# Two-layer transformer step, one core: the order of the matmuls of a pair of 64-wide heads in neighbourhood attention

## The chip, the core and the metric

The kernel runs on one core of one Trainium2 chip, in float32 throughout (many matmuls take float32 values that were rounded to the chip's fp32r form). The metric is device time in microseconds, the median of several executions; lower is better.

## The reference, cut to what matters

The program computes a first block (spatial gating, sparse attention, cross attention to a memory, feed-forward) and then a second block of two layers on a latent sequence `x` of 512 rows and a context `ctx` of 256 rows. The change touches only the attention of the second block: 8 heads of width 64. Each query of the latent grid (8 rows of 64 columns) sees a band of its grid neighbours and all 256 context rows; in layer 0 the context also attends to itself.

```python
def context_attention(q, k, v):
    s = jnp.einsum('bqhd,bkhd->bhqk', q, k, preferred_element_type=jnp.float32) * (NA_HEAD_DIM ** -0.5)
    p = jax.nn.softmax(s, axis=-1).astype(v.dtype)
    return jnp.einsum('bhqk,bkhd->bqhd', p, v).reshape(B, L, NA_CH)

def row_block(r):          # neighbourhood_attention, one grid row of queries
    ...
    s_loc = jnp.einsum('bjqhd,bijkhd->bhjqik', q_r, k_b,
                       preferred_element_type=jnp.float32) * scale + bias
    s_ctx = jnp.einsum('bjqhd,bchd->bhjqc', q_r, k_ctx,
                       preferred_element_type=jnp.float32) * scale
    s = jnp.concatenate([s_loc.reshape(B, NA_HEADS, nj, NA_QC, n_loc), s_ctx], axis=-1)
    p = jax.nn.softmax(s, axis=-1).astype(v.dtype)
    p_loc = p[..., :n_loc].reshape(B, NA_HEADS, nj, NA_QC, kh, NA_KB)
    o = (jnp.einsum('bhjqik,bijkhd->bjqhd', p_loc, v_b)
         + jnp.einsum('bhjqc,bchd->bjqhd', p[..., n_loc:], v_ctx))
```

## The kernel before, in words

The program is written as five instruction streams, one for each engine, by five functions that walk through the same stages in the same order; semaphores tie them together. The order on each engine is the order of the code. Most of the program on TensorE is large projections: a weight tile is split into a high and a low fp32r part (`hib` and `lob`), the activations likewise (`Hh` and `Hl`), and three matmuls (high by high, low by high, high by low) make one product. All matmuls go through the helper `mm` (line 816) and all transposes through `turn` (line 819), so the profile puts nearly all of TensorE's work on these two lines, and the tiles' names tell them apart.

The change lies in `near_attention` of TensorE's stream (line 1413). The work there is cut into pairs of heads: `hp` is one of four pairs of heads, `j` one of four blocks of 128 queries for the latent (`s == "x"`), or one of two for the context (`s == "c"`). That is 16 steps for `x` in each of the two layers and 8 steps for `c` in layer 0 only. The two heads of a pair, `b` = 0 and 1, lie side by side in the same buffers: head 0 on partitions 0 to 63, head 1 on partitions 64 to 127.

One step on TensorE, in this order (`by_pairs`, with a depth of 3 steps for `x` and 2 for `c`):

- `n_turn` of the pair three steps back (two for `c`): transposes of its softmax weights, eight (four for `c`), into a PSUM bank for each head (one for both in `c`).
- `n_scores` of this pair. For `x` each head's bank first gets a mask by a matmul with the identity (`near_maskr`). Then come the scores: queries `Hh`, `Hl` against keys `near_KH`, `near_KL`, three products, over 256 near keys and over 256 context keys for `x`, over the context keys alone for `c`. Each of these matmuls uses only the 64 partitions of its head as contraction, and each head writes its own bank. One semaphore increment behind the last matmul tells VectorE that both banks are full.
- Work from other parts ("beside"): 12 matmuls of a projection of 128x512 in many steps, in others nothing.
- `n_out` of the pair three steps back (two for `c`): the transposed weights (`near_PTt`, or `near_P` in `c`) against the values: four key blocks of 128 for `x` (two of `near_VB`, two of `near_VX`), two for `c` (`near_VX`). Here all 128 partitions are the contraction, each head has 64 output rows, and head `b` writes partitions 64b to 64b+63 of one shared bank. Each of these plain float32 matmuls leaves two records in the trace.

ScalarE copies the transposed weights of head 0 and then of head 1 out of PSUM (line 2208 ff., signal `pt2` for each head; in `c` one copy with both signals). VectorE adds the position bias and finds the row maximum (L3216, L3219), ScalarE takes the exponential with the row sum, and VectorE divides (L3229). In layer 1 and in the context stage VectorE also does the short convolutions and the pooling between these (L3104, L3115, L3134 to L3173).

Of the kernel before, what the change touches and what calls it, by code (L numbers as in the profile page):

```python
# [25 lines left out]
T = 512  # L26
TC = 256
# [22 lines left out]
BAND0 = [0, 8, 24, 32]  # L50
# [34 lines left out]
class Signals:  # L85
# [30 lines left out]
    def at(self, *key):  # L116
        if key[-1] is None:
            return None, 0
        if self.known is None:
            return None, 0  # L120
        found = self.known[key]
        return (None, 0) if found is None else (self.line(found[0]), found[1])
# [292 lines left out]
def near_pairs(s):  # L415

    return [(hp, j) for hp in range(4) for j in range(4 if s == "x" else 2)]
# [122 lines left out]
def program(nc, d, plan):  # L540
    ctx = ExitStack()
    with ctx:
        S = Signals(nc, ctx, plan)
        sig, at, mark, get = S.sig, S.at, S.mark, S.get
        chunks, units, P = sweeps(d)

        def sb(name, shape, dt=F32, where=None):
            return (where or ctx).enter_context(nc.sbuf_tensor(name, shape, dt))

        ps = ctx.enter_context(nc.psum_tensor("ps", [128, 8, 512], F32))  # L550
        X = sb("X", [128, 8, T])
        Hh = sb("Hh", [128, 8, T + TC], F32R)
        Hl = sb("Hl", [128, 8, T + TC], F32R)
# [204 lines left out]
        def query_at(H_, k, i):  # L758

            return H_[:, 2 * k + i // 2, T + 128 * (i % 2):T + 128 * (i % 2) + 128]  # L760

        def second_at(H_, k, s, j):

            return query_at(H_, k, j) if s == "x" else H_[:, 4 + k, T + 128 * j:T + 128 * j + 128]
# [34 lines left out]
        def tensor(e):  # L799
            w = Queue(e)  # L800
# [3 lines left out]
            def done(*keys):  # L804
                return sig("pe", *keys)
# [9 lines left out]
            def mm(out, lhsT, rhs, start, stop):  # L815
                return e.matmul(out, lhsT, rhs, start=start, stop=stop)  # L816
# [146 lines left out]
            def by_tile(name, some, acts, keep=False):  # L963

                s_ = P[name]
                got = {o: take("o", name, o) for o in s_.outs}
                for c in s_.chunks:
                    w.wait_ge(*at("lo", c.unit.u))
                    for o in s_.outs:
                        some(s_, c, o, acts, got, ([("full", name, o)] if c is s_.chunks[-1] else [])  # L970
                             + ([("used", c.unit.u)] if o == s_.outs[-1] else []))
                        if o == s_.outs[-1] and c is s_.chunks[-1] and not keep:
                            give_all(name)
                        yield
# [438 lines left out]
            def near_attention(l, s):  # L1413
                N = near[l]
                pairs = near_pairs(s)
                streams = {name: by_tile(name, fm_products, {"x": x_act(4 + 3 * l)}, True)
                           for what, name in sum(beside_pairs(l, s).values(), []) if what == "tile"}

                def near_out(bank):
                    return ps[:, bank, 0:256].rearrange("p (i c) -> p i c", c=32)  # L1420

                def near_keys(K_, r, hp, j):
                    return K_[r, hp, 0:T].rearrange("p (i c) -> p i c", c=64)[:, :, BAND0[j]:BAND0[j] + 32]

                def n_scores(p_):
                    hp, j = pairs[p_]
                    w.wait_ge(*at("q2", l, s, hp))
                    w.wait_ge(*at("k2", l, 1, (1, "c")))
                    got = [take("s2", l, s, p_, b) for b in range(2)]
                    for bank, before in got:  # L1430
                        freed(before)
                        if s == "x":
                            w.wait_ge(*at("maskr", l))
                            w.wait_ge(*at("identr"))
                            mm(ps[:, bank, 0:256], identr[:, :], N["maskr"][:, 256 * KIND[j]:256 * KIND[j] + 256], True, False)
                    halves = [slice(64 * b, 64 * b + 64) for b in range(2)]
                    products = [(Hh, N["KH"]), (Hh, N["KL"]), (Hl, N["KH"])]
                    far = slice(256, 512) if s == "x" else slice(0, TC)
                    for n, (H_, K_) in enumerate(products if s == "x" else []):
                        for (bank, _), r in zip(got, halves):  # L1440
                            mm(near_out(bank), second_at(H_, hp, s, j)[r], near_keys(K_, r, hp, j), False, n == 2)
                    for n, (H_, K_) in enumerate(products):
                        for (bank, _), r in zip(got, halves):
                            m = mm(ps[:, bank, far], second_at(H_, hp, s, j)[r], K_[r, hp, T:T + TC], n == 0, n == 2)
                    m.then_inc(*done(("scores2", l, s, p_)))
                    for b in range(len(got)):
                        give("s2", l, s, p_, b)

                def n_turn(p_):
                    n = 4 if s == "x" else 2  # L1450
                    got = [take("t2", l, s, p_, b) for b in range(2 if s == "x" else 1)]
                    w.wait_ge(*at("scaled2", l, s, p_))
                    for b in range(2):
                        bank, before = got[b % len(got)]
                        freed(before)
                        for k in range(n):
                            to = 128 * k + (0 if s == "x" else 256 * b)
                            m = turn(ps[:, bank, to:to + 128], weights_at(l, s, p_, b)[:, k // 2, 128 * (k % 2):128 * (k % 2) + 128])
                    m.then_inc(*done(("turned2", l, s, p_)))
                    for b in range(len(got)):  # L1460
                        give("t2", l, s, p_, b)

                def n_out(p_):
                    hp, j = pairs[p_]
                    bank, before = take("ot", l, s, p_)
                    freed(before)
                    w.wait_ge(*at("vb", l))
                    w.wait_ge(*at("vx", l, 1))
                    nk = 4 if s == "x" else 2
                    for k in range(nk):  # L1470
                        for b in range(2):
                            h = 2 * hp + b
                            w.wait_ge(*at("pt2", l, s, p_, b))
                            if s == "x" and k < 2:
                                vv = N["VB"][:, j, k, 64 * h:64 * h + 64]
                            else:
                                vv = N["VX"][:, k % 2, 64 * h:64 * h + 64]
                            m = mm(ps[64 * b:64 * b + 64, bank, 0:128], vv, turned_keys(l, s, p_, b)[:, 128 * k:128 * k + 128],
                                   k == 0, k == nk - 1)
                    m.then_inc(*done(("pout2", l, s, p_)))  # L1480

                def n_final(p_):
                    give("ot", l, s, p_)

                def beside_do(what, n):
                    if what == "tile":
                        next(streams[n])
                        if n == ("conv", l, "x", 2) and l == 1:
                            mark("pe", "hfree", "x", l)
                    elif what == "project":  # L1490
                        project(l, "x", n)
                    elif what == "out":
                        next(outs[n])
                    elif what == "projected":
                        give("pw", l, "x", n)
                    elif what == "project c":
                        project(l, "c", n)
                    elif what == "projected c":
                        give("pw", l, "c", n)
                    elif what == "conv":  # L1500
                        give_all(("conv", l, "x", n))
                    elif what == "pooled":
                        give("o", ("pool", l, "x"), (n, "x"))
                    elif what == "added":
                        give_all((("out2", l, 0), "x", n))
                outs = [by_tile((("out2", l, 0), "x", pair), fm_products, mixed_acts(l), l == 0 or pair == 0) for pair in range(4)]
                by_pairs(len(pairs), [n_turn, n_scores, "beside", n_out, n_final],
                         [depth(s), 0, 0, depth(s), depth(s) + 1], beside_pairs(l, s), beside_do)
                return outs
# [2060 lines left out]
```

## Time and profile before

| | |
|---|---|
| median of 3 runs | 3359.93 us (3359.46 to 3360.32) |
| the profiled execution | 3359.93 us, its span 3358.1 us |
| TensorE matmul busy | 3240.9 us, 97% of the span, 18042 records |
| VectorE busy | 2495.7 us, 74% |
| ScalarE busy | 1275.7 us, 38% |
| GpSimd busy | 629.3 us, 19% |
| mean granted TensorE clock | 0.988 |

The profiled execution took the same time as the median; 1.8 us of it lie outside the span. The time of a matmul in the trace runs from its start to the end of its last result, and matmuls are pipelined, so the records of neighbours overlap: what a matmul costs the engine is the distance from one start to the next, not its own duration. In the views that merge records, a row gives the start of the first one, the time from there to the end of the last one, and how many there are. The three attention stages lie at about 1435 to 1502 us (`c`, layer 0), 1545 to 1634 us (`x`, layer 0) and 2829 to 2943 us (`x`, layer 1).

### The profile page before, as it was taken

What the parts mean: (1) busy time and instruction counts of PE and PEld (TensorE: products, weight loads), DVE (VectorE), ACT (ScalarE), POOL (GpSimd) and SP (SyncE); (2) the same over time, 40 slices, a digit from 0 to 9 for tenths busy, and PEclk for the clock granted to TensorE, in tenths of its full rate; (3) what the DMA queues carried; (4) which work ended last, traced back from release to release, by engine and by line L of the source; (5) the groups of instructions that cost most, each with busy time, mean ns of one, the idle gap of its engine ahead of it and who ended that gap; (6) DMA issues with size and microseconds to landing.
All of it is one profiled execution on the core that took longest, in us unless ns stands there. A gap on an engine that the chain in (4) does not pass through costs nothing. (4 is left out here: it accounts for less than half of the span.)

```text
span 3358.1 us, 45852 instructions
## 1 busy us (share of the span) xinstructions
PE 3240.9 (97%) x18042; PEld 2875.5 (86%) x18042; DVE 2495.7 (74%) x4610; ACT 1275.7 (38%) x2257; POOL 629.3 (19%) x657
## 2 busy tenths in 40 slices
PE   7989999999999999999999999999999989999998
PEld 6788778888999998978799999989999978788887
DVE  5576678888889898576788889888999965753333
ACT  4475543333332334334533332443332343432222
POOL 0100011112522221301052222143222213100000
PEclk9999999999999999999999999999999999999999
DMA  5201245564233333523113333323333333123332
GB/s 169 63 26 47 79 157 184 170 188 142 70 119 110 113 98 106 152 88 95 60 57 111 119 110 107 99 75 93 109 110 114 97 119 96 50 82 99 96 99 77
DMA packets 381929, 348.90 MB, mean 104 GB/s; under 512 B 17440, under 2 KB 338336, under 8 KB 381200
## 3 DMA queue, kind: packets, MB, share of 16 engines
q1 hardware_dynamic: 337696, 250.74, 24.6%
q0 software_dynamic: 17232, 46.84, 4.7%
q10 hardware_dynamic: 26784, 48.37, 4.6%
q8 instruction: 142, 2.33, 0.3%
q14 instruction: 75, 0.61, 0.1%
HBM read 339.60 MB, written 2.10 MB: 102 GB/s over the span
## 5 line engine op out<-in xcount | busy, mean ns | idle before, releaser
L816 PE MATMUL ps<-Hh,hib 128*128 128x512 f32 (+2 forms) x2672 | 955.7, 358 | 15.3 <-DVE Hl L2501 6.4
L816 PE MATMUL ps<-Hl,hib 128*128 128x512 f32 (+2 forms) x2672 | 947.0, 354 | 0.0
L816 PE MATMUL ps<-Hh,lob 128*128 128x512 f32 (+2 forms) x2672 | 946.5, 354 | 0.0
L2369 DVE TENSOR_TENSOR lob<-rawb,hib 128x1024 fp32r<-128x1024 f32 (+2 forms) x361 | 442.2, 1229 | 383.9 <-ACT hib L1597 382.0
L1597 ACT ACTIVATE hib<-rawb 128x1024 fp32r<-128x1024 f32 (+2 forms) x589 | 508.3, 872 | 573.4 <-PE ps L816 568.3
L816 PEld LDWEIGHTS ps<-Hh,hib 128*128 128x128 f32 x2672 | 507.9, 190 | 78.3 <-DVE Hl L2501 11.8
L816 PEld LDWEIGHTS ps<-Hh,lob 128*128 128x128 f32 x2672 | 507.9, 190 | 52.5
L816 PEld LDWEIGHTS ps<-Hl,hib 128*128 128x128 f32 x2672 | 508.4, 190 | 49.4 <-issue 0.5
L816 PE MATMUL ps<-Gha,hib 128*128 128x512 f32 (+1 forms) x704 | 238.5, 339 | 5.1 <-DVE lob L2369 3.7
L816 PE MATMUL ps<-Gla,hib 128*128 128x512 f32 (+1 forms) x704 | 237.2, 337 | 0.0
L816 PE MATMUL ps<-Gha,lob 128*128 128x512 f32 (+1 forms) x704 | 236.7, 336 | 0.0
L2371 DVE TENSOR_TENSOR lob<-rawb,hib 128x512 fp32r<-128x512 f32 x228 | 224.2, 993 | 10.5 <-ACT hib L1597 10.3
L3007 DVE TENSOR_TENSOR Tm<-Tm,ps 128x384 f32<-128x384 f32 x399 | 216.4, 548 | 6.3
L816 PE MATMUL ps<-Ghb,hib 128*128 128x512 f32 (+1 forms) x528 | 187.8, 356 | 2.0 <-DVE lob L2369 1.7
L816 PE MATMUL ps<-Glb,hib 128*128 128x512 f32 (+1 forms) x528 | 187.1, 354 | 0.0
L816 PE MATMUL ps<-Ghb,lob 128*128 128x512 f32 (+1 forms) x528 | 186.8, 354 | 0.0
L2394 DVE CUSTOM_DVE_ANT_0 MRa<-MRa 128x512 f32<-128x512 f32 x234 | 183.0, 833 | 3.0 <-DMA MRa<-in_w_mod_t 3.0
L816 PE MATMUL ps<-Eha,hib 128*128 128x384 f32 x456 | 153.0, 336 | 6.7 <-DVE lob L2371 6.7
L816 PEld LDWEIGHTS ps<-Gha,hib 128*128 128x128 f32 x704 | 133.6, 190 | 22.2 <-DVE lob L2369 5.9
L816 PE MATMUL ps<-Ela,hib 128*128 128x384 f32 x456 | 152.4, 334 | 0.0
L816 PE MATMUL ps<-Eha,lob 128*128 128x384 f32 x456 | 152.4, 334 | 0.0
L2551 DVE SCALAR_TENSOR_TENSOR X<-ps,CF,X 128x512 f32<-128x512 f32 x176 | 124.9, 742 | 28.8 <-PE ps L816 28.7
(329 smaller groups left out, 5763.9 us busy)
## 6 DMA issues: line engine op xcount, KB each, us to landing
rawb<-in_ffn_w_in SPq DMA_DIRECT2D x114, 512.0 KB, 3.8
rawb<-in_ffn_w_out SPq DMA_DIRECT2D x76, 512.0 KB, 3.4
rawb<-in_w_in SPq DMA_DIRECT2D x74, 512.0 KB, 3.6
rawb<-in_w_ff SPq DMA_DIRECT2D x64, 512.0 KB, 3.7
rawb<-in_ffn_w_in SPq DMA_DIRECT2D x124, 256.0 KB, 3.3
MRa<-in_w_mod_t ACTq DMA_DIRECT2D x117, 256.0 KB, 3.1
MR<-in_w_mod_t POOLq DMA_DIRECT2D x112, 256.0 KB, 3.5
MRb<-in_w_mod_t ACTq DMA_DIRECT2D x59, 256.0 KB, 3.0
```

Source lines behind the costliest of these rows:

```text
L816: return e.matmul(out, lhsT, rhs, start=start, stop=stop)
L1597: return e.activation(out, src, f, **k)
L2369: e.tensor_tensor(lob_of(x.chunk), raw_of(x.chunk), hib_of(x.chunk), ALU.subtract).then_inc(*done(("lo", x.u)))
L2371: e.tensor_tensor(by_q(half_of(lob, x)), weights_source(x.cross.name[0], x), by_q(half_of(hib, x)), ALU.subtract).then_inc(*done(("lo", x.u)))
L2394: e.tensor_tensor_reduce(row if q else mod_junk[turn], row, scb[:, q, h, :], 1.0, 0.0, ALU.mult, ALU.add, to).then_inc(*done(*([("modused" ...
L2551: m = e.scalar_tensor_tensor(o, y, cf, o, ALU.mult, ALU.add)
L3007: e.tensor_tensor(slot(to), a, b, op).then_inc(*done(*keys))
```

## The change

Within a step, the matmuls of the two heads are no longer alternated. `n_scores` now issues all of head 0's products (three near, three context) and then all of head 1's, and `n_out` all of head 0's key blocks and then all of head 1's. The masks, the transposes, the banks, the number and the shapes of the matmuls and the semaphore increments are the same. In `n_out`, the wait for head 1's copied weights now stands behind all of head 0's matmuls and no longer behind the first of them.

```diff
-                    halves = [slice(64 * b, 64 * b + 64) for b in range(2)]
-                    products = [(Hh, N["KH"]), (Hh, N["KL"]), (Hl, N["KH"])]
-                    far = slice(256, 512) if s == "x" else slice(0, TC)
-                    for n, (H_, K_) in enumerate(products if s == "x" else []):
-                        for (bank, _), r in zip(got, halves):
-                            mm(near_out(bank), second_at(H_, hp, s, j)[r], near_keys(K_, r, hp, j), False, n == 2)
-                    for n, (H_, K_) in enumerate(products):
-                        for (bank, _), r in zip(got, halves):
-                            m = mm(ps[:, bank, far], second_at(H_, hp, s, j)[r], K_[r, hp, T:T + TC], n == 0, n == 2)
+                    for b in range(2):
+                        r = slice(64 * b, 64 * b + 64)
...
+                        if s == "x":
+                            bank = got[b][0]
+                            scores(ps[:, bank, 0:256].rearrange("p (i c) -> p i c", c=32), q_, near_keys, False)
+                            m = scores(ps[:, bank, 256:512], q_, context_keys, True)
+                        else:
+                            m = scores(ps[:, got[b][0], 0:TC], q_, context_keys, True)
...
-                    for k in range(nk):
-                        for b in range(2):
-                            h = 2 * hp + b
-                            w.wait_ge(*at("pt2", l, s, p_, b))
+                    for b in range(2):
+                        w.wait_ge(*at("pt2", l, s, p_, b))
+                        h = 2 * hp + b
+                        nk = 4 if s == "x" else 2
+                        for k in range(nk):
```

`scores` is a new helper of three `mm` calls in a row: `Hh` by `KH`, `Hh` by `KL`, `Hl` by `KH`.

TensorE, end of a latent step of layer 0 and start of the next, before. `near_VB` and `near_VX` hold the values, `near_PTt` the transposed weights, `near_KH` and `near_KL` the keys; a row with x2 is two matmuls of one kind, here one for each head, and "waits act" is a wait for ScalarE's copy:

```order
L816 MATMUL ps<-near_PTt,near_VB 64x128 [waits act] x2
L816 MATMUL ps<-near_PTt,near_VB 64x128 x2
L816 MATMUL ps<-near_PTt,near_VX 64x128 x4
L819 MATMUL ps<-con,near_P 128x128 [waits dve]
L819 MATMUL ps<-con,near_P 128x128 x7
L816 MATMUL ps<-near_maskr,identr 128x256
L816 MATMUL ps<-near_maskr,identr 128x256 [waits act]
L816 MATMUL ps<-near_KH,Hh 128x256 x2
L816 MATMUL ps<-near_KL,Hh 128x256 x2
L816 MATMUL ps<-near_KH,Hl 128x256 x2
L816 MATMUL ps<-near_KH,Hh 128x256 x2
```

The first two rows are key blocks 0 and 1, heads alternating; the third row is four matmuls for two blocks and two heads.

TensorE, the `n_out` part of the same place, after the change:

```order
L816 MATMUL ps<-near_PTt,near_VB 64x128 [waits act]
L816 MATMUL ps<-near_PTt,near_VB 64x128
L816 MATMUL ps<-near_PTt,near_VX 64x128 x2
L816 MATMUL ps<-near_PTt,near_VB 64x128 [waits act]
L816 MATMUL ps<-near_PTt,near_VB 64x128
L816 MATMUL ps<-near_PTt,near_VX 64x128 x2
```

Head 0's four matmuls stand together, then the second wait, then head 1's four.

TensorE, the `n_scores` part behind the masks, after the change:

```order
L816 MATMUL ps<-near_KH,Hh 128x256
L816 MATMUL ps<-near_KL,Hh 128x256
L816 MATMUL ps<-near_KH,Hl 128x256
L816 MATMUL ps<-near_KH,Hh 128x256
L816 MATMUL ps<-near_KL,Hh 128x256
L816 MATMUL ps<-near_KH,Hl 128x256
L816 MATMUL ps<-near_KH,Hh 128x256
L816 MATMUL ps<-near_KL,Hh 128x256
L816 MATMUL ps<-near_KH,Hl 128x256
L816 MATMUL ps<-near_KH,Hh 128x256
L816 MATMUL ps<-near_KL,Hh 128x256
L816 MATMUL ps<-near_KH,Hl 128x256
```

The first six are head 0's (near, then context), the last six head 1's. No other engine's order changes.

## Rows read from the trace of the kernel before

**Rows 1.** Busy time by stage: the three attention stages (engine columns: us busy, records)

```profile
core 0: us, PE busy (x) PEld busy (x) DVE busy (x) ACT busy (x) POOL busy (x), PEclk, DMA share, GB/s
1435.00:1502.00 67.00, 63.10 (x354) 48.19 (x354) 51.29 (x127) 26.42 (x66) 0.00 (x0) 1.00 0.25 79
1545.00:1634.00 89.00, 80.75 (x713) 64.29 (x712) 65.25 (x150) 50.86 (x124) 15.56 (x32) 1.00 0.15 40
2829.00:2943.00 114.00, 105.57 (x809) 83.68 (x808) 81.17 (x176) 54.95 (x128) 15.83 (x32) 0.97 0.16 43
```

**Rows 2.** Groups of instructions by shape, TensorE, the whole program

```profile
L816 PE MATMUL ps<-near_KH,Hh 64*128 64x256 f32 x144 | 24.7, 339 | 1.7 <-DVE Hl L3190 0.9 <-DVE Tm L3104 0.8
L816 PE MATMUL ps<-near_PTt,near_VB 128*64 128x128 f32 x256 | 24.0, 286 | 6.9 <-ACT near_PTt L1597 6.8
L816 PE MATMUL ps<-near_P,near_VX 128*64 128x128 f32 x64 | 5.3, 285 | 1.5 <-ACT near_P L1597 1.5
```

**Rows 3.** Order of time, TensorE, one latent step of layer 0 (start, length)

```profile
1561.72 0.66 PE L816 MATMUL ps<-near_PTt,near_VB 128*64 128x128 f32 x8
1562.21 0.61 PE L816 MATMUL ps<-near_PTt,near_VX 128*64 128x128 f32 x8
1562.75 1.09 PE L819 MATMUL ps<-con,near_P 128*128 128x128 f32 x8
1563.60 0.48 PE L816 MATMUL ps<-near_maskr,identr 128*128 128x256 f32 x2
1564.00 0.39 PE L816 MATMUL ps<-near_KH,Hh 64*128 64x256 f32 x2
1564.23 0.29 PE L816 MATMUL ps<-near_KL,Hh 64*128 64x256 f32 x2
1564.35 0.28 PE L816 MATMUL ps<-near_KH,Hl 64*128 64x256 f32 x2
1564.47 0.28 PE L816 MATMUL ps<-near_KH,Hh 64*128 64x256 f32 x2
1564.59 0.28 PE L816 MATMUL ps<-near_KL,Hh 64*128 64x256 f32 x2
1564.71 0.28 PE L816 MATMUL ps<-near_KH,Hl 64*128 64x256 f32 x2
1564.92 0.50 PE L816 MATMUL ps<-Hh,hib 128*128 128x512 f32 x1
```

**Rows 4.** Order of time, TensorE, 128x256 products of a projection

```profile
1430.06 0.28 PE L816 MATMUL ps<-Hh,lob 128*128 128x256 f32 x1
1430.18 0.28 PE L816 MATMUL ps<-Hh,hib 128*128 128x256 f32 x1
1430.30 0.28 PE L816 MATMUL ps<-Hl,hib 128*128 128x256 f32 x1
```

**Rows 5.** Order of time, TensorE, the context step's `n_out`

```profile
1455.89 0.66 PE L816 MATMUL ps<-near_P,near_VX 128*64 128x128 f32 x8
```

**Rows 6.** Order of time, weight loads, the same step as rows 3

```profile
1564.11 0.19 PEld L816 LDWEIGHTS ps<-near_KL,Hh 64*128 64x128 f32 x2
```

**Rows 7.** Waits, latent stage of layer 0 (us in total, times, longest)

```profile
PE ps L816 <- ACT near_PTt L1597: 4.1, 5, 1.5
PE ps L816 <- DVE Hl L3181: 2.2, 2, 2.0
PE ps L816 <- ACT near_P L1597: 0.6, 2, 0.3
...
DVE ps L3216 <- PE ps L816: 8.7, 9, 1.6
```

**Rows 8.** Waits, latent stage of layer 1

```profile
PE ps L816 <- ACT near_PTt L1597: 5.7, 2, 3.0
PE ps L816 <- DVE Tm L3104: 1.3, 1, 1.3
PE ps L816 <- DVE near_PV L3173: 0.8, 1, 0.8
PE ps L816 <- ACT near_P L1597: 0.5, 2, 0.3
```

**Rows 9.** Order of time, TensorE, the last `n_out` of layer 0

```profile
1631.63 1.03 PE L816 MATMUL ps<-near_PTt,near_VB 128*64 128x128 f32 x7 [0.69 <-ACT near_PTt L1597]
...
1632.50 0.70 PE L816 MATMUL ps<-near_PTt,near_VX 128*64 128x128 f32 x7
```

**Rows 10.** Order of time, ScalarE, the same place

```profile
1630.98 1.08 ACT L1597 ACTIVATE near_PTt<-ps 128x512 f32<-128x512 f32 x2 [2.03 <-PE ps L819]
```

**Rows 11.** Busy time in one stretch of layer 1 (columns as rows 1)

```profile
2919.70:2923.00 3.30, 3.30 (x19) 2.74 (x16) 2.54 (x6) 2.23 (x7) 0.00 (x0) 0.50 0.02 5
```

More of the change, by code:

```diff
@@ L1417, in near_attention, with scores @@
                            for what, name in sum(beside_pairs(l, s).values(), []) if what == "tile"}
[L1419 to L1423, printed above, removed]
+                def scores(out, q_, k_, first):
+                    mm(out, q_(Hh), k_(N["KH"]), first, False)
+                    mm(out, q_(Hh), k_(N["KL"]), False, False)
+                    return mm(out, q_(Hl), k_(N["KH"]), False, True)
                 def n_scores(p_):
@@ L1429, in n_scores @@
                     got = [take("s2", l, s, p_, b) for b in range(2)]
-                    for bank, before in got:
+                    for b, (bank, before) in enumerate(got):
                         freed(before)
@@ L1435, in n_scores, with q_, near_keys, context_keys @@
                             mm(ps[:, bank, 0:256], identr[:, :], N["maskr"][:, 256 * KIND[j]:256 * KIND[j] + 256], True, False)
-                    halves = [slice(64 * b, 64 * b + 64) for b in range(2)]
-                    products = [(Hh, N["KH"]), (Hh, N["KL"]), (Hl, N["KH"])]
-                    far = slice(256, 512) if s == "x" else slice(0, TC)
-                    for n, (H_, K_) in enumerate(products if s == "x" else []):
-                        for (bank, _), r in zip(got, halves):
-                            mm(near_out(bank), second_at(H_, hp, s, j)[r], near_keys(K_, r, hp, j), False, n == 2)
-                    for n, (H_, K_) in enumerate(products):
-                        for (bank, _), r in zip(got, halves):
-                            m = mm(ps[:, bank, far], second_at(H_, hp, s, j)[r], K_[r, hp, T:T + TC], n == 0, n == 2)
+                    for b in range(2):
+                        r = slice(64 * b, 64 * b + 64)
+                        def q_(H_):
+                            return second_at(H_, hp, s, j)[r]
+                        def near_keys(K_):
+                            return K_[r, hp, 0:T].rearrange("p (i c) -> p i c", c=64)[:, :, BAND0[j]:BAND0[j] + 32]
+                        def context_keys(K_):
+                            return K_[r, hp, T:T + TC]
+                        if s == "x":
[4 more added lines that the diff above has]
+                            m = scores(ps[:, got[b][0], 0:TC], q_, context_keys, True)
                     m.then_inc(*done(("scores2", l, s, p_)))
@@ L1468, in n_out @@
                     w.wait_ge(*at("vx", l, 1))
-                    nk = 4 if s == "x" else 2
-                    for k in range(nk):
-                        for b in range(2):
-                            h = 2 * hp + b
-                            w.wait_ge(*at("pt2", l, s, p_, b))
+                    for b in range(2):
[3 more added lines that the diff above has]
+                        for k in range(nk):
                             if s == "x" and k < 2:
```

## The prediction

> **What bounds the kernel now.** The summary of the page puts TensorE's matmuls at 97% of the span, so I read first how far this holds where the change is: the table of busy time by stage [rows 1]. In the three attention stages TensorE is busy for 63.1 of 67 us, 80.75 of 89 and 105.57 of 114. VectorE, the next engine, is busy for 51.3, 65.3 and 81.2. The reader is to see two things. TensorE sets the pace in each of the stages, and all its idle time there is 3.9 + 8.25 + 8.43 = 20.6 us: that is the most that could hide an addition to TensorE's work.
>
> The second view is the groups by shape, for the counts [rows 2]. The first product of the scores has 144 records: 2 layers x 16 latent steps x 2 heads x 2 (near and context), that is 128, and 8 context steps x 2 heads = 16. The third view is the order of time in one step, and everything hangs on it [rows 3]. There the score matmuls stand in rows of x2, and the rows start at 1564.23, .35, .47, .59 and .71: two matmuls of 256 columns every 0.12 us. An ordinary projection with the same 256 columns and all 128 partitions starts one matmul every 0.12 us [rows 4]. So two heads' matmuls, which lie on different halves of the partitions and write different banks, go through the engine at the same time, and a pair costs what one costs.
>
> The same holds for the output matmuls, where the heads share the partitions but use different halves of the array's columns. Sixteen records last from 1561.72 to 1562.21 + 0.61 = 1562.82, that is 1.10 us [rows 3]. Eight transposes of the same 128 columns, which can't be paired, last 1.09 us; take off one record's own length, about 0.29 us [rows 2], and seven distances of 0.11 us are left [rows 3]. One after another, sixteen records would need 15 x 0.11 + 0.29 = 1.94 us. They take 1.10, so here too they run two at a time: eight slots of 0.11 us, not sixteen.
>
> **The change part by part.** It adds and removes no instruction. It takes apart the neighbours that run together: behind a matmul of head 0 now comes another of head 0, which needs the same part of the array, and so has to wait for its turn.
>
> Scores, latent step: 12 matmuls in 6 slots before. After it, head 0's six take six slots. Head 0's last and head 1's first are neighbours and lie on different halves, so I let these two still run together: 6 + 6 - 1 = 11 slots. Five slots more x 0.12 us = 0.60 us; 32 steps make 19.2 us. If the hand-over doesn't overlap, it is 12 slots and 0.12 us more in a step.
>
> Scores, context step: 6 matmuls in 3 slots, after it 5. Two slots x 0.12 us x 8 steps = 1.9 us.
>
> Output, latent step: 16 records in 8 slots before, after it 8 + 8 - 1 = 15. Seven slots x 0.11 us = 0.77 us; 32 steps make 24.6 us. Without the overlap at the hand-over 0.11 us more in a step.
>
> Output, context step: 8 records, which last 0.66 us now [rows 5], in 4 slots; after it 7. Three x 0.11 us x 8 = 2.6 us.
>
> Gross: 19.2 + 1.9 + 24.6 + 2.6 = 48.3 us. The trace has no row with two matmuls of 64 partitions one after another on the same half. But each half's own stream has one in every 0.12 us already, since the x2 rows are two such streams side by side, and that pace is all that the sum uses.
>
> One rule speaks for a much higher price. The row: the weights of `near_KL` are being loaded from 1564.11 [rows 6] while the matmul of `near_KH` on the same half, which began at 1564.00, is still running until 1564.39 [rows 3]. So the loading for the next matmul of a half lies under the present one. The Trainium skill says in "TensorE: Matmul & The Clock Gate", section "The mechanism" (packing of small matmuls), that a weight load overlaps running matmuls only where the row group differs. By that rule each slot of one half would have to hold load and matmul in turn. The trace disagrees here: the load goes to the same row group.
>
> What hides a part of the 48.3 us: time in which TensorE waits for something that its own delay doesn't push back.
>
> Latent stage of layer 0, opening: three score groups stand back to back, and then TensorE waits 2.0 us for VectorE [rows 7]. VectorE starts with the first group, so that delay counts, and the other two vanish in the wait: 2 x 0.6 = 1.2 us.
>
> Latent stage of layer 0, the last seven output steps. No projection lies between transposes and outputs there, so TensorE waits for ScalarE's copy, 4.1 us in five waits [rows 7]. In the last step ScalarE's two copies take 1.08 us together [rows 10], and TensorE starts at 1631.63, with the first copy, and ends at 1632.50 + 0.70 = 1633.20 [rows 9]: 1.57 us instead of 1.10, because head 1's first matmul waits for the second copy and holds back head 0's. After the change head 0's four matmuls (eight records, 0.88 us) run in that time, and about 0.47 us of the 0.77 is had back. The pattern stands in seven steps, in three of them fully, with about 0.4 us in two and 0.2 in two more: 2.6 us. Two of the five waits stand behind scores and also swallow their 0.6 us, at most 1.0 us in all, and the waits for freed banks (0.6 us, `near_P`) swallow as much: 4.2 us.
>
> Context stage: the releasers of its waits are VectorE's halves and convolutions, 0.9 and 0.8 us at the scores [rows 2] and some more at the projections; I take off 1.0 us.
>
> Latent stage of layer 1: the waits for convolution and pooling (1.3 and 0.8 us) hide one output step's 0.77 each; the wait of 3.0 us hides one group of scores, 0.6; the banks 0.5; the last wait for copies, 0.5 [rows 8]: 3.1 us. The rest of these waits comes from chains that begin with TensorE's own scores. VectorE waited for them 9 times in layer 0 [rows 7], and what TensorE is late there comes back.
>
> In sum 1.2 + 4.2 + 1.0 + 3.1 = 9.5 us are hidden, and 48.3 - 9.5 = 38.8 us are left. At 1.2 GHz stands one stretch in the stages, 3.3 us at a granted clock of 0.50 behind a wait in layer 1 [rows 11]. It costs about half of its length. The wait in front of it stays, and so I leave this cost where it is: if it went, 1.7 us would come back; the work now in it gets longer by under 1 us. I add nothing for it and round to 39 us. The profiled execution took 3359.93 us, exactly the median, so nothing is corrected: 3359.9 + 39 = **3399 us**, 1.2% slower.
>
> **The rivals.**
>
> *No overlap at the hand-over.* One slot more in each group: 32 x (0.12 + 0.11) + 8 x 0.23 = 9.2 us, so 48 us and 3408. For it speaks that the trace shows pairs only where both streams ran in step; against it, that two neighbours on different halves is all that the x2 rows are.
>
> *All of TensorE's idle time hides it.* 48.3 - 20.6 = 27.7 us, 3388 us. For it: VectorE has idle time too and could catch up [rows 1]. Against it: most waits of layer 0 lie at its two ends [rows 7], where they can't serve the steps between, and VectorE itself waits for the scores.
>
> *Weights can't be loaded beside a running matmul of the same half.* Then each slot is as the first of a group, 1564.00 to 1564.23, 0.23 us instead of 0.12 [rows 3]. 11 slots x 0.11 us = 1.2 us more for the scores in 32 steps, 0.55 in 8, and if the outputs' slots grew as much, 1.65 and 0.8: about 100 us more, 3500; with the scores alone 43 more, 3442. This is what the rule above would give. Against it stand rows 6.
>
> *Not slower.* The engine looks ahead and starts head 1's matmuls beside head 0's, whatever the order. Then the slots are as before, and of the change is left only the later wait in `n_out`, which gives back 2.6 us in layer 0 and 0.5 in layer 1 (from the above): 3357 us. It decides from the point where the engine can start a matmul three places down the queue (six for the scores). For it: the loads are seen to run ahead of the matmuls. Against it: in the staggered outputs of the last step, head 0's `near_VX` blocks were free to go four slots behind 1631.63, at 1632.07, and stand at 1632.50, behind head 1's first ones [rows 9]. The Trainium skill says in "TensorE: Matmul & The Clock Gate", section "The mechanism", that matmuls start and end in the program's order, and by that this rival falls; the trace agrees by that row.
>
> **How the numbers follow.** Forecast 0.66; no overlap at the hand-over 0.14; all idle time hides it 0.11; loads not hidden 0.04; not slower 0.05. The forecast's own range is 3392 to 3405: a third more or less of the 9.5 us hidden, and 3% of slot length. The range takes in the two rivals beside it: 3386 to 3411. That leaves out the last two and the tails. A measurement of this kernel tells 0.2%, some 7 us, from no change. Slower by more than that is everything but the last rival: 0.95. Within it 0.03 and faster 0.02 share the last one, since 3357 is inside the bound.
>
> **What would show each step.** In the order of time, single rows of 64x256 score matmuls 0.12 us apart, with one x2 at the middle of each group; the group lasts 1.3 us from first to last start instead of 0.71. Output groups of latent steps last 1.87 us instead of 1.10, with the second head's first record beside the first head's last. Undisturbed latent steps get 0.60 + 0.77 = 1.37 us longer. The stages grow by about 4 us (context), 17 (layer 0) and 19 (layer 1), and the rest of the program by nothing; waits for ScalarE's copies before the outputs shrink, while the total of TensorE's busy time grows by more than 40 us. I am wrong if x2 rows are still there all through, or if single rows stand 0.23 us apart.

## The result and the profile after

The changed kernel takes 3380.03 us (3378.93 to 3380.56, 4 runs) against 3359.69 us before (3358.57 to 3360.32, 4 runs): a ratio of 1.0055, 95% interval 1.0042 to 1.0068. That is 20 us slower. I had forecast 39 and a range that ended at 26 us: the sign was right, the size was not, and one step of the sum was wrong by its mechanism.

Single times of one kernel spread by some 10 us (the kernel before reaches from 3356 to 3370 us over all series), so the sharper measure is the length of the three attention stages in the trace. Busy time by stage, each from its first score matmul or mask to the end of its last output (columns as in [rows 1]). The kernel before, its two latent stages and the sum of all three:

```profile
1545.87:1633.25 87.38, 79.13 (x706) 62.95 (x705) 64.68 (x147) 50.11 (x123) 15.56 (x32) 1.00 0.15 37
2829.24:2942.33 113.09, 104.66 (x806) 82.92 (x805) 80.88 (x175) 54.29 (x126) 15.83 (x32) 0.97 0.16 43
sum 265.48, PE 245.84 PEld 193.02 DVE 196.02 ACT 128.88 POOL 31.39; mean PE 81.95 PEld 64.34 DVE 65.34 ACT 42.96 POOL 10.46
```

The changed kernel:

```profile
1438.30:1503.49 65.19, 62.24 (x345) 47.24 (x346) 50.56 (x124) 24.48 (x61) 0.00 (x0) 1.00 0.25 78
1548.35:1643.39 95.04, 91.19 (x706) 75.95 (x705) 64.94 (x147) 50.05 (x123) 15.52 (x32) 0.98 0.13 34
2837.13:2960.26 123.13, 117.19 (x806) 95.93 (x805) 81.11 (x175) 54.16 (x127) 15.53 (x32) 0.97 0.14 40
sum 283.36, PE 270.62 PEld 219.12 DVE 196.61 ACT 128.69 POOL 31.05; mean PE 90.20 PEld 73.04 DVE 65.54 ACT 42.90 POOL 10.35
```

The stages together are 17.9 us longer, of the 18.9 us by which the span grew. VectorE's and ScalarE's busy time is the same to 1 us. The context stage has grown by only 0.2 us: 65.2 us, where the kernel before has 65.0. The latent stages grew by 7.7 and 10.0 us.

One latent step of the changed kernel, the scores, in order of time on TensorE (start, length); it answers to [rows 3]:

```profile
1567.29 0.38 PE L816 MATMUL ps<-near_KH,Hh 64*128 64x256 f32 x1
1567.52 0.28 PE L816 MATMUL ps<-near_KL,Hh 64*128 64x256 f32 x1
1567.64 0.28 PE L816 MATMUL ps<-near_KH,Hl 64*128 64x256 f32 x1
1567.65 0.39 PE L816 MATMUL ps<-near_KH,Hh 64*128 64x256 f32 x2
1567.87 0.28 PE L816 MATMUL ps<-near_KL,Hh 64*128 64x256 f32 x2
1567.99 0.28 PE L816 MATMUL ps<-near_KH,Hl 64*128 64x256 f32 x2
1568.12 0.27 PE L816 MATMUL ps<-near_KH,Hh 64*128 64x256 f32 x1
1568.23 0.28 PE L816 MATMUL ps<-near_KL,Hh 64*128 64x256 f32 x1
1568.35 0.28 PE L816 MATMUL ps<-near_KH,Hl 64*128 64x256 f32 x1
```

Three single rows, three rows of x2, three single rows. In the program head 0's six stand ahead of head 1's six. So the pairs in the middle are head 0's last three with head 1's first three, and head 1 started right behind head 0's third, while three of head 0's were still to come: the row at 1567.65 begins 0.01 us behind the one at 1567.64, too soon for another matmul of the same half, which follows 0.12 us later. From first to last start it is 1.06 us: nine slots of 0.12, where there were six [rows 3] and I had expected eleven.

The outputs of the step before it:

```profile
1564.53 0.65 PE L816 MATMUL ps<-near_PTt,near_VB 128*64 128x128 f32 x4
1565.02 0.27 PE L816 MATMUL ps<-near_PTt,near_VX 128*64 128x128 f32 x1
1565.02 0.32 PE L816 MATMUL ps<-near_PTt,near_VB 128*64 128x128 f32 x1
...
1565.51 0.60 PE L816 MATMUL ps<-near_PTt,near_VX 128*64 128x128 f32 x4
```

Head 0's four `near_VB` records, and then `near_VX` (still head 0) and `near_VB` (already head 1) side by side from 1565.02. Head 1 starts beside head 0's fifth record of eight. The group lasts from 1564.53 to 1566.11, 1.58 us instead of 1.10 [rows 3]; I had expected 1.87. A context step, the scores and the outputs:

```profile
1452.04 0.39 PE L816 MATMUL ps<-near_KH,Hh 64*128 64x256 f32 x2
1452.26 0.29 PE L816 MATMUL ps<-near_KL,Hh 64*128 64x256 f32 x2
1452.38 0.28 PE L816 MATMUL ps<-near_KH,Hl 64*128 64x256 f32 x2
...
1458.30 0.66 PE L816 MATMUL ps<-near_P,near_VX 128*64 128x128 f32 x8
```

Here the rows are as before: x2 all through, and 0.66 us for the outputs [rows 5], although the program now gives three of head 0 and then three of head 1 (four records each in the outputs). In the context steps such a block costs nothing.

The waits in the latent stage of layer 0, where [rows 7] stood before, and in that of layer 1, where [rows 8] stood (us in total, times, longest). Layer 0:

```profile
PE ps L816 <- ACT near_PTt L1604: 2.5, 3, 1.2
PE ps L816 <- DVE Hl L3188: 1.0, 1, 1.0
```

Layer 1:

```profile
PE ps L816 <- ACT near_PTt L1604: 4.5, 2, 2.7
PE ps L816 <- DVE Tm L3111: 0.8, 1, 0.8
PE ps L816 <- DVE near_PV L3180: 0.3, 1, 0.3
```

All of these have shrunk: time that hid a part of the longer groups. One more wait of layer 0 before, the 1.2 us before the first transposes for VectorE's weights, is not in this list. In its place TensorE ran for 3.4 us at a granted clock of 0.51, that is at 1.2 GHz, after the wait of 1.0 us (1554.90 to 1558.30), and came to the transposes just as late: 10.7 us into the stage, before and after. So the slow stretch is no part of the 17.9 us. Nor is what layer 1 has of such stretches, since it is 6.8 us both before (from 2848.0 and from 2919.7, 3.4 us each) and after (2855.3 to 2862.1).

### The profile page after: what moved, and what is told of

The parts are those of the page before. It is cut to its first block and busy times, and to the rows that moved or that the text cites. A ratio compares the mean times of both kernels' runs of the same rounds, so it can differ in the third digit from the quotient of the medians.

```text
span 3377.0 us, 45852 instructions
## 1 busy us (share of the span) xinstructions
PE 3265.8 (97%) x18042; PEld 2901.4 (86%) x18042; DVE 2493.1 (74%) x4610; ACT 1275.4 (38%) x2257; POOL 628.6 (19%) x657
```

## The experiments

The theory after this reading: the engine takes matmuls in order, but each half of the array (by partitions for the scores, by columns for the outputs) works through its own, and a matmul for the idle half may start as soon as no more than three matmuls ahead of it have not yet started. The rival is the one of my prediction: only two neighbours at the hand-over run together.

### Scores alone, outputs alone

In the first, `n_scores` is that of the changed kernel and `n_out` that of the kernel before; in the second it is the other way round.

```diff
 e1: - for n, (H_, K_) in enumerate(products): for (bank, _), r in zip(got, halves): ...
     + for b in range(2): scores(near keys); scores(context keys)
 e2: - for k in range(nk): for b in range(2): wait pt2(b) ...
     + for b in range(2): wait pt2(b); for k in range(nk): ...
```

> Only the scores are grouped by head, the outputs alternate as before. Theory (a head on another half of the array may start once only three matmuls of the head in front of it have not started): head 1's first score matmul of a latent step starts beside head 0's third or fourth, the group lasts 1.05 us from first to last start instead of 0.71, context steps stay at three rows of x2; 0.35 us x 32 steps = 11 us gross, about 8 us slower than before, some 3368 us. Rival (only the two matmuls at the hand-over run together, as I predicted): the group lasts 1.3 us, context steps grow by 0.24 us; 19 + 2 us gross, about 16 us slower.

> Only the outputs are grouped by head, the scores alternate as before. Theory: head 1's first output record starts beside head 0's fifth, the group of a latent step grows from 1.10 to 1.58 us, context steps don't grow; 0.49 us x 32 = 16 us gross, less some 3 us at the stages' ends, where head 0 no longer waits behind head 1's copy: about 12 us slower, 3372 us. Rival (only the hand-over overlaps): group 1.87 us, 25 + 3 us gross, about 23 us slower.

Scores alone: 3371.71 us, ratio 1.0030 (1.0019 to 1.0042). Outputs alone: 3370.41 us, ratio 1.0028 (1.0019 to 1.0037). The sums of the three stages, the first kernel:

```profile
sum 274.00, PE 257.71 PEld 204.53 DVE 196.67 ACT 128.78 POOL 31.05; mean PE 85.90 PEld 68.18 DVE 65.56 ACT 42.93 POOL 10.35
```

and the second:

```profile
sum 274.35, PE 257.94 PEld 206.89 DVE 196.54 ACT 128.86 POOL 31.30; mean PE 85.98 PEld 68.96 DVE 65.51 ACT 42.95 POOL 10.43
```

The stages grow by 8.5 and by 8.9 us; together 17.4, nearly the 17.9 of the whole change. For the scores the theory's 8 us holds. For the outputs it is 3 us less than I had expected: of their 0.48 x 32 = 15.4 us gross 6.5 are hidden, where I had put some 3. The rival's 16 and 23 us are out.

### Blocks of three

```diff
+for (bank, _), r in zip(got, halves):
+    for n, (H_, K_) in enumerate(products):      # three of one head, then three of the other
 ...
+for k0 in range(0, nk, 2):
+    for b in range(2):
+        wait pt2(b)
+        for k in (k0, k0 + 1):                   # two key blocks, four records
```

> Heads alternate in blocks: three score matmuls of head 0, three of head 1, and so on; two key blocks (four records) of outputs each. Theory: no block is longer than what may stand waiting in front, so scores keep 0.71 us and outputs 1.10 us a step, and the later wait in the outputs gives back about 2 us at the ends of the stages: 0 to 3 us faster than before, 3357 to 3360 us. Rival (neighbours on different halves run together, others don't): scores 9 slots and outputs 13 instead of 6 and 8, 0.36 + 0.55 us a latent step, 29 us gross, about 22 us slower.

3364.56 us, ratio 1.0010 (1.0000 to 1.0019). The stages:

```profile
sum 266.63, PE 247.31 PEld 195.76 DVE 196.22 ACT 128.88 POOL 31.30; mean PE 82.44 PEld 65.25 DVE 65.41 ACT 42.96 POOL 10.43
```

1.2 us more than before in the stages (3.3 in whole time), where the rival wanted 22. The scores are again six rows of x2 in 0.71 us. The small gain that I had expected is not there. One output group of this kernel:

```profile
1560.95 0.66 PE L816 MATMUL ps<-near_PTt,near_VB 128*64 128x128 f32 x8
1561.43 0.66 PE L816 MATMUL ps<-near_PTt,near_VX 128*64 128x128 f32 x8
```

It lasts to 1562.09, 1.14 us instead of 1.10. In 32 steps that is 1.3 us. So the pairs are all kept, but a block of four records isn't quite free here.

### The depth: five and one, and twelve

These two kernels ran once each and serve only for the start of head 1. In the first, five matmuls of head 0 and five of head 1 are followed by the last of each. In the second, each product of the latent scores is issued twice, so that twelve stand against twelve.

```diff
 e8: +for some in (near_ + far_[:2], far_[2:]):   # five, then one
     +    for (bank, _), r in zip(got, halves):
     +        for n, near_by in some: mm(...)
 e5: +for twice in range(2): scores(near keys)
     +for twice in range(2): m = scores(context keys)
```

> Scores of latent steps in blocks of five and one: five matmuls of head 0, five of head 1, then the last one of each; outputs as before. Theory (depth of three): head 1 starts with head 0's second matmul, 0.22 us behind the first, and the group lasts 0.93 us, between the 0.71 of blocks of one or three and the 1.06 of six. Rival (halfway): 0.25 to 0.35 us behind the first, group 0.95 to 1.05 us.

> The changed kernel with each score product of the latent steps issued twice (twelve matmuls of head 0, then twelve of head 1; the products count double, so the output is not the reference's). Theory (fixed depth: head 1 may start once three matmuls of head 0 have not started): it starts with head 0's ninth, 1.05 us behind the first, and the group lasts 2.46 us from first to last start. Rival (it starts halfway, whatever the number): 0.7 to 0.8 us behind the first, group 2.1 to 2.2 us. Two interleaved streams of twelve would need 1.4 us.

Their single times are 3370.52 us (five and one) and 3418.52 us (twelve), beside a median of 3362.26 us before; nothing is built on them. Five and one, order of time on TensorE:

```profile
1562.10 0.39 PE L816 MATMUL ps<-near_KH,Hh 64*128 64x256 f32 x1
1562.32 0.29 PE L816 MATMUL ps<-near_KL,Hh 64*128 64x256 f32 x1
1562.33 0.38 PE L816 MATMUL ps<-near_KH,Hh 64*128 64x256 f32 x1
...
1563.03 0.28 PE L816 MATMUL ps<-near_KH,Hl 64*128 64x256 f32 x1
```

Head 1's first (the second `near_KH,Hh`) stands at 1562.33, beside head 0's second, and the last start is 0.93 us behind the first, as the theory has it. Twelve against twelve:

```profile
1561.10 0.39 PE L816 MATMUL ps<-near_KH,Hh 64*128 64x256 f32 x1
...
1562.17 0.28 PE L816 MATMUL ps<-near_KH,Hl 64*128 64x256 f32 x1
1562.18 0.39 PE L816 MATMUL ps<-near_KH,Hh 64*128 64x256 f32 x2
...
1562.52 0.29 PE L816 MATMUL ps<-near_KH,Hl 64*128 64x256 f32 x2
...
1563.59 0.28 PE L816 MATMUL ps<-near_KH,Hl 64*128 64x256 f32 x1
```

Nine single rows up to 1562.17, three of x2, nine single ones: head 1 starts with head 0's ninth, 1.08 us behind the first, and the group lasts 2.49 us. "Halfway" would have been 0.7 to 0.8 and 2.1 to 2.2. So it is a fixed number and no share. In one table, head 1's start behind head 0's first:

| head 0's block | starts beside its | behind its first |
|---|---|---|
| 3 matmuls, or 4 records | first | 0.01 us |
| 5 | second | 0.23 us |
| 6 (the change, scores) | third, just behind it | 0.36 us |
| 8 records (the change, outputs) | fifth | 0.49 us |
| 12 | ninth | 1.08 us |

In each row from four records on exactly three of head 0's have not started when head 1 does. The lead of head 0 in the last column is also what a latent group gets longer by: 1.06 instead of 0.71 us for six, 1.58 instead of 1.10 for eight records. Whether the three are places in a queue of each half or in one for the whole engine was not tested.

### The same half

```diff
-halves = [slice(64 * b, 64 * b + 64) for b in range(2)]
+halves = [slice(0, 64) for b in range(2)]
```

> The order of before, but the scores of both heads read the partitions 0 to 63, so head 1's scores are head 0's and the output is not the reference's. Theory (the pairs run together because they use different halves, not because of their order): 12 slots of 0.12 us instead of 6 in a latent step and 6 instead of 3 in a context step: 0.71 x 32 + 0.36 x 8 = 26 us gross, 18 to 22 us slower than before, about 3380 us. It is the price of losing the pairs of the scores altogether. Rival (any two neighbouring matmuls of 64 partitions overlap): no difference.

3384.09 us, ratio 1.0064 (1.0050 to 1.0078); the stages:

```profile
sum 287.24, PE 272.00 PEld 219.50 DVE 196.97 ACT 128.63 POOL 31.30; mean PE 90.67 PEld 73.17 DVE 65.66 ACT 42.88 POOL 10.43
```

21.8 us more than before in the stages, within the 18 to 22, and 22.8 in whole time. Some 1.3 us of it, by the starts on either side, come from 3.4 us at a granted clock of 0.51 near the end of layer 0 (1635.80 to 1639.20), where the kernel before stands at full clock. The order is that of before, but each x2 row now holds its two matmuls one behind the other, and the rows start 0.24 us apart:

```profile
1567.23 0.40 PE L816 MATMUL ps<-near_KL,Hh 64*128 64x256 f32 x2
1567.47 0.40 PE L816 MATMUL ps<-near_KH,Hl 64*128 64x256 f32 x2
```

So what makes two score matmuls run together is that they use different halves of the partitions; for the halves of the columns, in the outputs, no such kernel was made. This is also the price of losing the scores' pairs altogether. The grouped scores of the change lost only three of six in a latent step and none in a context step, and paid 8.5 us for it.

### Both waits first

```diff
+for b in range(2):
+    w.wait_ge(*at("pt2", l, s, p_, b))
 for b in range(2):
-    w.wait_ge(*at("pt2", l, s, p_, b))
     h = 2 * hp + b
```

> The changed kernel, but the outputs wait for both heads' copied weights before head 0's first matmul, as the kernel before in effect did. It prices what the later wait gives back. Theory: where TensorE waits for the copies at the ends of the stages, some 0.5 us come back in each of about seven steps of layer 0 and one or two of layer 1: 2 to 4 us slower than the changed kernel, about 3384 us where the changed kernel has 3381. Rival (the later wait gives nothing, what is hidden comes from elsewhere): the same time as the changed kernel.

The stages:

```profile
sum 287.63, PE 270.69 PEld 219.60 DVE 196.64 ACT 128.91 POOL 31.04; mean PE 90.23 PEld 73.20 DVE 65.55 ACT 42.97 POOL 10.35
```

4.3 us more than the changed kernel (283.36), just above the 2 to 4 of the theory. In layer 0 it is 2.25 us (97.29 against 95.04), and that is the waits' doing. The last step of layer 0 shows it, first with both waits in front,

```profile
1639.66 0.62 PE L816 MATMUL ps<-near_PTt,near_VB 128*64 128x128 f32 x4 [1.27 <-ACT near_PTt L1605]
```

and then the changed kernel:

```profile
1641.77 0.65 PE L816 MATMUL ps<-near_PTt,near_VB 128*64 128x128 f32 x4 [0.69 <-ACT near_PTt L1604]
```

TensorE waits 1.27 us for the copies instead of 0.69. In layer 1 it is 2.12 us (125.25 against 123.13), and only 0.5 of that is the wait itself (2.32 us instead of 1.84 at one place). The other 1.6 come behind it, where this kernel ran at 1.2 GHz for 3.4 us, and the changed kernel did the same work at full clock (first both waits in front, then the changed kernel; the last figures but two are the granted clock):

```profile
2935.20:2938.60 3.40, 3.40 (x21) 3.07 (x17) 2.39 (x6) 1.64 (x6) 0.00 (x0) 0.50 0.02 5
2936.40:2939.80 3.40, 3.40 (x36) 2.96 (x32) 2.97 (x8) 2.20 (x7) 0.00 (x0) 1.00 0.02 5
```

That leaves 2.8 us for what the later wait itself hides, and the slow stretch behind the longer wait makes the rest; whether the longer wait brought it about was not tested. In whole time (3380.32 us, ratio 1.0056, 1.0043 to 1.0070) the two kernels can't be told apart (3380.03 and, once more, 3379.11 us for the changed one); by this measure alone the experiment would be inconclusive.

### The change once more, and one block ahead

The changed kernel again, in the same series as a last variant, which keeps the scores of before and lets head 0's outputs run one key block ahead. The edit shown is that of the last variant; the changed kernel is unaltered.

```diff
+turns = [(0, 0), (0, 1), (1, 0), (0, 2), (1, 1), (0, 3), (1, 2), (1, 3)]
+for b, k in [x for x in turns if x[1] < nk]:
```

> The changed kernel once more, beside the others and in the same rounds as the kernel before, since single times of one kernel spread over some 10 us. The three attention stages together 283 to 284 us against 265.5 before, 18 us; in whole time 0.5 to 0.6% slower. If the 18 us were an accident of one trace, the stages would come out otherwise.

> The kernel before with head 0's outputs one key block ahead: head 0's blocks 0 and 1, then head 1's 0, head 0's 2, head 1's 1, and so on; scores as before. Theory: never more than three matmuls of one head stand in front of the other, so a group of outputs keeps 0.82 us between first and last start, and where TensorE waits for the copies, head 0's four records run while head 1's copy is made: 0.3 to 0.45 us back in about seven steps of layer 0 and one of layer 1, the stages together 262 to 264 us instead of 265.5. In whole time 0 to 3 us faster than before, which the rounds can hardly tell. Rival (any departure from strict alternation costs): groups of 0.9 us or more, stages over 267 us.

The changed kernel: 3379.11 us, ratio 1.0055 (1.0041 to 1.0069), and its stages

```profile
sum 283.41, PE 269.19 PEld 218.43 DVE 196.69 ACT 128.87 POOL 31.05; mean PE 89.73 PEld 72.81 DVE 65.56 ACT 42.96 POOL 10.35
```

agree with the first trace to 0.05 us, although layer 0 has no slow stretch this time and the wait before the first transposes is there, 1.3 us. One block ahead: 3362.50 us, ratio 1.0001 (0.9992 to 1.0010), stages

```profile
sum 266.07, PE 246.83 PEld 195.60 DVE 196.15 ACT 128.69 POOL 31.31; mean PE 82.28 PEld 65.20 DVE 65.38 ACT 42.90 POOL 10.44
```

0.6 us longer than before and not 1.5 to 3.5 shorter. An output group, which I had expected to stay at 1.10 us:

```profile
1565.40 0.71 PE L816 MATMUL ps<-near_PTt,near_VB 128*64 128x128 f32 x8
1565.89 0.66 PE L816 MATMUL ps<-near_PTt,near_VX 128*64 128x128 f32 x8
```

takes 1.15 us. That is 1.6 us in 32 steps, more than the waits give back here. In the trace these 0.05 us lie in a single slot of head 1, of 0.15 us instead of 0.11. Why was not tried apart and stays open. No version was found that beats the kernel before.

## Why the prediction was wrong

**What bounds the kernel**: right. TensorE sets the pace in the latent stages, and the cost of the longer groups arrived there; outside the three stages the spans differ by 1 us. (The range of the forecast alone, 3392 to 3405, is wider than its own two terms, which give about 5 us to either side; the measured time lies outside both.)

**Pairs run together before**: right, from the x2 rows [rows 3], and shown for the scores by the kernel with both heads on one half, which pays 21.8 us. A half's own pace is 0.12 us, as the sum had it: the single rows above are 0.12 us apart, and the loading of weights lies under the running matmul of the same half [rows 6]. The Trainium skill's rule against this ("TensorE: Matmul & The Clock Gate", section "The mechanism"), that a weight load overlaps running matmuls only where the row group differs (the section excepts loads into a background weight buffer), would have meant 0.23 us by the prediction's reading. No run shows that but in the first distance of a group.

**The hand-over costs all slots but one**: this is the step that failed. I wrote "Head 0's last and head 1's first are neighbours and lie on different halves, so I let these two still run together: 6 + 6 - 1 = 11 slots". Head 1 passes three waiting matmuls or records, so a group gets longer only by head 0's lead up to there. Three of six pairs are left in the scores and four of eight in the outputs, and all of them in the context steps. With the lengths from the traces:

| group | forecast | measured |
|---|---|---|
| scores, latent | + 0.60 us | + 0.35 us (0.71 to 1.06) |
| outputs, latent | + 0.77 us | + 0.48 us (1.10 to 1.58) |
| scores, context | + 0.24 us | none |
| outputs, context | + 0.33 us | none |

Gross that is (0.35 + 0.48) x 32 = 26.6 us instead of 48.3. The miss of 21 us in the stages lies here, with 21.7 us too much gross; what is hidden came out 0.8 us smaller than forecast.

**What is hidden**: right in size, in part by luck. 26.6 - 17.9 = 8.7 us, where I had 9.5 with the context's 1.0. By stage: 13.3 - 7.7 = 5.6 in layer 0 (forecast 5.4) and 13.3 - 10.0 = 3.3 in layer 1 (forecast 3.1). But the forecast's terms were worked out with 0.60 and 0.77 us a group. With the measured 0.35 and 0.48 the same terms give only some 4.6 in layer 0 (0.7 + 2.6 + 0.7 + 0.6) and 2.3 in layer 1 (0.96 + 0.35 + 0.5 + 0.5), 6.9 us in all. That is an estimate, but by it the waits swallowed more than I had seen: at the opening of layer 0 all three groups of scores vanish and not two, since the first transposes come 10.7 us into the stage both before and after. That the later wait is a part of it is shown, with some 2.8 us against 3.1 forecast; how the rest divides over the single waits was only read from shrunken waits and not tested.

**The rival "not slower"** had the true mechanism in it, a look ahead, and I gave it 0.05 because of a row that I misread. In [rows 9] head 0's later blocks stood still behind head 1's first, and I took that to mean that nothing passes a waiting matmul. But head 1's was waiting for a semaphore, not for its half of the array, and that wait held everything behind it: head 0's third record starts only with head 1's first, at 1632.12, right behind the end of ScalarE's second copy at 1632.06 [rows 10]. The same trace before, the first row from a narrower window:

```profile
1632.12 0.33 PE L816 MATMUL ps<-near_PTt,near_VB 128*64 128x128 f32 x2
...
1632.39 0.27 PE L816 MATMUL ps<-near_PTt,near_VX 128*64 128x128 f32 x1
1632.49 0.27 PE L816 MATMUL ps<-near_PTt,near_VB 128*64 128x128 f32 x1
```

The last two rows stood in the place of the dots in [rows 9] and were a hint that I passed over. In the program every `near_VB` record stands in front of every `near_VX` one, and here a `near_VX` record starts 0.10 us ahead of the last `near_VB`. It is only the second record of a matmul that is passed, so it proves little by itself; the groups of the changed kernel show the passing in full. I also put the look ahead as all or nothing: from three places down the queue in the outputs, or six in the scores, all slots were to be as before. It reaches three, and half of the pairs were kept. The Trainium skill's sentence, in the same section ("TensorE: Matmul & The Clock Gate", "The mechanism"), that matmuls start and end in the program's order had seemed to settle it. The traces disagree: in the twelve against twelve, head 1's first starts at 1562.18 and head 0's tenth, which stands before it in the program, 0.11 us later.

Between nearly none and all of the pairs kept, my cases stood at 11 or 12 slots and at 6. A look ahead of limited depth lies between them, and I priced none.

## What to carry to other kernels

Two small matmuls that use different halves of the array, by their 64 partitions or their 64 output rows, ran at the price of one if no more than three matmuls of the one stood in front of the other, where a plain float32 matmul counts as its two records. Strict alternation isn't needed, but blocks of five and more lose pairs, and the loss grows with the block: 0.23 us for five, 0.36 for six, 1.08 for twelve. When a queue is seen to hold something back, ask whether what stands in front waits for a signal or only for the unit: the two behave differently. Where whole times spread by more than the effect, compare the lengths of the stages concerned, and the granted clock in them: one stretch of 3.4 us at 1.2 GHz moved a stage by 1.6 us here.

## What the runs showed of the hardware that I had not expected

A matmul for the idle half of the array starts ahead of up to three matmuls that stand before it in the program and wait for the busy half. The number was three for 256 columns at 0.12 us a slot and for records of 128 columns at 0.11 us, in blocks of 5, 6, 8 and 12. A half that gets its first matmul late takes a slot of 0.22 us for it, as the first one of a group does (1567.29 to 1567.52, and 1567.65 to 1567.87). A wait for a semaphore, in contrast, held back what stood behind it on the other half too (the row at 1632.12 above). And the stages' length is far steadier than the whole time: two traces of the changed kernel agree to 0.05 us in it (283.36 and 283.41), while single whole times of it reach from 3375 to 3383 us.
